# Relative-bias lines of two attention layers: kept with heads innermost, copied DRAM to DRAM, loaded as one run per partition and turned into head order by ScalarE

## What is computed

```
# first block: 16 heads, banded causal attention, window 128
s    = q.k + bias1[head, query - key]           # 128 queries x 256 keys, per block of 128 tokens
bias1[head, d] = rel_bias_table[bucket(d), head]  for 0 <= d < 128, else -1e30
# second block: 8 heads, three branches (compressed, selected, window)
s    = q.k + bias2[head, query - key]           # bucket(d), d < 512
# each block ends in a feed-forward over experts: 128 pairs of rows of two tables per token
```

## Time and profile before

| | |
|---|---|
| time, median of 3 runs | 3303.84 us (3301.78 to 3305.36) |
| the profiled execution | 3307.08 us, of which 3305.4 us are the span from first to last instruction |
| TensorE busy | 2453.2 us (74%) |
| VectorE busy | 2321.0 us (70%) |
| ScalarE busy | 1333.8 us (40%) |
| GpSimd busy | 1137.5 us (34%) |
| moved by DMA | 1295.01 MB, mean 392 GB/s |

### The profile page before, as it was taken

One profiled execution on the slowest core, in us unless ns is written; L12 is line 12 of the kernel. 1 busy time (PEld: TensorE's weight loads), 2 busy tenths in 40 slices (PEclk: granted clock), 3 DMA queues, 4 the chain that ended last, 5 costly groups with the idle time before them and its releaser, 6 DMA issues.

```text
span 3305.4 us, 40579 instructions
## 1 busy us (share of the span) xinstructions
PE 2453.2 (74%) x14052; PEld 1044.4 (32%) x14052; DVE 2321.0 (70%) x5500; ACT 1333.8 (40%) x3603; POOL 1137.5 (34%) x1038
## 2 busy tenths in 40 slices
PE   8969679786797777879688769778876655555555
PEld 3533333223332233346343426423333211111111
DVE  7439783878838787475975685888866777777644
ACT  2114442444424443243483343368733333333322
POOL 0012332324323243332343343444433444443432
PEclk9979879897898978989888979878888777777777
DMA  8899999999999999999999999999999999999997
GB/s 243 310 354 414 412 375 394 411 402 406 382 406 418 412 401 396 408 371 404 369 380 384 386 396 391 408 418 416 385 405 361 414 418 416 417 410 414 420 420 323
DMA packets 214057, 1295.01 MB, mean 392 GB/s; under 512 B 26934, under 2 KB 30294, under 8 KB 82776
## 3 DMA queue, kind: packets, MB, share of 16 engines
q0 software_dynamic: 148320, 1076.50, 80.7%
q1 hardware_dynamic: 64860, 213.81, 17.1%
q10 hardware_dynamic: 672, 2.12, 0.2%
HBM read 1289.62 MB, written 2.71 MB: 391 GB/s over the span
## 4 chain that ended last, share of the span: by engine, by line
PE 34%; DMA 26%; DVE 22%; issue 9%; ACT 5%; POOL 3%; SPq 0%; POOLq 0%; DVEq 0%; ACTq 0%
PE ps L1718 10%; DMA ring<-in_k_vu,idx 10%; PE ps L1798 10%; DMA ring<-in_k_uv,idx 9%; DVE ring L415 9%; DMA wsl<-in_k_wu 5%; PE ps L2092 5%; POOL ring L2396 3%; ACT L1245 2%; PE ps L2102 2%; DVE big L470 2%; PE ps L1775 1%; PE ps L1973 1%; ACT diag L1245 1%; DMA wsl<-in_k_wmod 1%
## 5 line engine op out<-in xcount | busy, mean ns | idle before, releaser
L1718 PE MATMUL ps<-ring,diag 64*64 64x512 f32 x8192 | 1257.7, 742 | 487.3 <-ACT diag L1245 464.4
L415 DVE CUSTOM_DVE_ANT_0 ring<-ring,xn 128x1024 f32<-128x1024 f32 x1024 | 1238.3, 1221 | 480.6 <-DMA ring<-in_k_vu,idx 268.5
L2396 POOL DMA_INDIRECT ring<-in_k_vu,idx x514 | 566.1, 1101 | 1147.0 <-DVE aw L415 663.1
L2396 POOL DMA_INDIRECT ring<-in_k_uv,idx x510 | 565.2, 1108 | 946.3 <-DVE aw L415 674.4
L1718 PEld LDWEIGHTS ps<-ring,diag 64*64 64x64 f32 x8192 | 313.2, 158 | 1259.9 <-ACT diag L1245 739.7
L1245 ACT ACTIVATE aw<-aw 128x2 f32<-128x2 f32 x512 | 104.2, 204 | 1077.1 <-DVE aw L415 1075.8
L1798 PE MATMUL ps<-wsl,xT 128*128 128x512 f32 x896 | 429.2, 622 | 30.5 <-DMA wsl<-in_k_wu 26.5
L1245 ACT ACT_TABLE_LOAD x340 | 436.2, 1283 | 21.2 <-issue 9.3
L1245 ACT ACTIVATE diag<-gid,aw 128x64 f32<-128x64 f32 x1024 | 311.9, 343 | 308.3 <-PE ps L1718 292.3
L1245 ACT ACTIVATE gid<-ident,gate 128x64 f32<-128x64 f32 x1024 | 293.9, 335 | 0.0
L1798 PEld LDWEIGHTS ps<-wsl,xT 128*128 128x128 f32 x896 | 165.7, 196 | 291.9 <-issue 228.3
(11 more groups left out here) (264 smaller groups left out, 2155.2 us busy)
## 6 DMA issues: line engine op xcount, KB each, us to landing
wsl<-in_k_wu SPq DMA_DIRECT2D x342, 512.0 KB, 9.8
wsl<-in_k_wmod SPq DMA_DIRECT2D x40, 512.0 KB, 6.2
ring<-in_k_vu,idx POOLq DMA_INDIRECT x514
ring<-in_k_uv,idx POOLq DMA_INDIRECT x510
ring<-in_k_wmod SPq DMA_DIRECT2D x8, 512.0 KB, 10.4
wsl<-in_k_wu SPq DMA_DIRECT2D x8, 280.0 KB, 19.2
hres<-in_x SPq DMA_DIRECT2D x4, 512.0 KB, 5.9
pers<-L1d POOLq DMA_DIRECT2D x8, 256.0 KB, 15.8
```

The costliest lines, as they stand in the source:

```text
L415: V(v.tensor_tensor_reduce(u_row(s), u_row(s), xn[:, n % 3, :], 1.0, 0.0, ALU.mult, ALU.add, aw[:, b, k:k + 1]), ("dot", s))
L1718: r = t.matmul(PA[half][64 * q:64 * q + 64, :], diag[64 * half:64 * half + 64, s % (2 * PAIR), :], v_row(s)[64 * half:64 * half + 64, 512 ...
L2396: Q(p.indirect_dma_start(out=both_rows(s), out_offset=None, in_=tab, in_offset=bass.IndirectOffsetOnAxis(ap=idx[:, n % 2, k:k + 1], axis=0 ...
```

## The change

The line is now made with distances on the partitions: three matmuls of 128 distances each, heads as columns (so a [128, 3, heads] tile), and the mask is a [128, 3] column tile. The line goes to DRAM once (`lined`, mark `line`), distance by distance with the heads innermost. A second transfer copies it inside DRAM 16 times, end to end (`copied`, rows of 384 x heads). From there the row of a query, all heads, is one contiguous run: 16 KB for block one, 8 KB for block two. Eight transfers of 16 partitions each bring it to `raw1` (scratch in the ring) or `raw2`, key-major with the heads innermost. ScalarE then copies it into `bias1` (four copies of 8 heads x 128 keys, ahead of its evacuation of block b = 3) and `bias2` (two copies of 4 heads x 256 keys, behind the gates of tile pair 4). The loads of `raw1` no longer wait for block b = 3; they start when the copies have landed. VectorE's waits for `bias` become waits for `biased`.

```
-        def shifted(copies, heads, a):
-            return bass.AP(tensor=copies.tensor, offset=128 - 16 * a, ap=[[WC, 16], [16 * WC, heads], [1, 256]])
-        def copied(copies, heads):
-            return bass.AP(tensor=copies.tensor, offset=1, ap=[[16 * WC, heads], [WC + 1, 16], [1, W1]])
+        def shifted(blk, a):
+            nh = (16, 8)[blk]
+            return bass.AP(tensor=copied[blk].tensor, offset=(127 - 16 * a) * nh, ap=[[(W1 - 1) * nh, 16], [1, 256 * nh]])
...
+            def bias_turned(blk, raw, to, h0, k0, nk, part):
+                S.stage("bias")
+                S.wait_ge("bias", blk)
+                S(act(to[:, h0:h0 + 8 - 4 * blk, k0:k0 + nk], raw[:, k0:k0 + nk, h0:h0 + 8 - 4 * blk].rearrange("p k h -> p h k"),
+                      ACT.Copy), ("biased", blk, part))
...
+                    if b == 3:
+                        for part in range(4):
+                            bias_turned(0, raw1, bias1, 8 * (part % 2), 128 * (1 - part // 2), 128, part)
...
-                T(t.matmul(PS[0][0:nh, 0:W1], B["tb"][0:32, 0:nh], B["oh"][0:32, :], start=True, stop=True),
-                  ("bias_mm", blk))
+                for c in range(3):
+                    r = t.matmul(PS[0][:, nh * c:nh * c + nh], B["oh"][0:32, 128 * c:128 * c + 128], B["tb"][0:32, 0:nh],
+                                 start=True, stop=True)
+                T(r, ("bias_mm", blk))
...
-            G.wait_ge("bias_lv", 0)
-            lv = BB[0]["lv"][0:16, 0:W1]
-            Q(p.dma_start(copied(L1d, 16), bc(lv.unsqueeze(1), [16, 16, W1])), "bias_d0", ("bias_d", 0))
-            G.wait_ge("bias_lv", 1)
-            lv = BB[1]["lv"][0:8, 0:W1]
-            Q(p.dma_start(copied(L2d, 8), bc(lv.unsqueeze(1), [8, 16, W1])), "bias_d1", ("bias_d", 1))
+            for blk, nh in ((0, 16), (1, 8)):
+                G.wait_ge("bias_lv", blk)
+                Q(p.dma_start(lined[blk].rearrange("c p h -> p c h"), BB[blk]["lv"][:, :, 0:nh]), "line%d" % blk, ("line", blk))
+            for blk, nh in ((0, 16), (1, 8)):
+                G.wait_ge("line", blk)
+                line = lined[blk].rearrange("c p h -> (c p h)")
+                Q(p.dma_start(copied[blk], bc(line.unsqueeze(0), [16, W1 * nh])), "bias_d%d" % blk, ("bias_d", blk))
             G.wait_ge("bias_d", 0)
-            G.wait_ge("win", 0, 3)
             for a in range(8):
-                Q(p.dma_start(bias1[16 * a:16 * a + 16, :, :], shifted(L1d, 16, a)), "bias0",
-                  *([("bias", 0)] if a == 7 else []))
+                Q(p.dma_start(raw1[16 * a:16 * a + 16, :, :], shifted(0, a)), "bias0", *([("bias", 0)] if a == 7 else []))
...
-                    Y.wait_ge("bias_d", 0)
-                    Y.wait_ge("bias_d", 1)
+                    Y.wait_ge("line", 1)
+                    Y.wait_ge("biased", 0, 3)
...
-                        Q(s.dma_start(bias2[16 * a:16 * a + 16, :, :], shifted(L2d, 8, a)), "bias1",
+                        Q(s.dma_start(raw2[16 * a:16 * a + 16, :, :], shifted(1, a)), "bias1",
```

More of the change, by code:

```diff
@@ L169, in build @@
         iob = bc(iot[:, :].unsqueeze(1).unsqueeze(1), [128, 2, 16, 16])
-        L1d = nc.dram_tensor("L1d", [16, 16, WC], F32, kind="Internal").ap()
-        L2d = nc.dram_tensor("L2d", [8, 16, WC], F32, kind="Internal").ap()
+        lined = [nc.dram_tensor("line%d" % k, [3, 128, nh], F32, kind="Internal").ap() for k, nh in enumerate((16, 8))]
+        copied = [nc.dram_tensor("copies%d" % k, [16, W1 * nh], F32, kind="Internal").ap() for k, nh in enumerate((16, 8))]
         modd = nc.dram_tensor("modd", [12, 512], F32, kind="Internal").ap()
@@ L299, in bias_bufs @@
             r["oh"], o = carve(base, o0, w)
-            r["mk"], o = carve(base, o, w)
+            r["mk"], o = carve(base, o, 3)
             r["tb"], o = carve(base, o, 16)
-            r["lv"], o = carve(base, o, w)
+            r["lv"], o = carve(base, o, 3, 16)
             return r
+        raw1 = carve(rflat, 11264, 256, 16)[0]
+        raw2 = carve(pers, at_route + 256, 256, 8)[0]
         BB = [bias_bufs(rflat, 3328, W1), bias_bufs(rflat, 4608, W1)]
@@ L568, in make_bias @@
                 V.wait_ge("bias_mk", blk)
-                V(tt(B["lv"][0:nh, :], PS[0][0:nh, 0:W1], B["mk"][0:nh, :], ALU.add), ("bias_lv", blk))
+                V(tt(B["lv"][:, :, 0:nh], PS[0][:, 0:3 * nh].rearrange("p (c h) -> p c h", c=3),
+                     bc(B["mk"].unsqueeze(2), [128, 3, nh]), ALU.add), ("bias_lv", blk))
             def norm1(n):
@@ L611, in first_tile @@
                     V.wait_ge("a_sc", 0, e)
-                    V.wait_ge("bias", 0)
+                    V.wait_ge("biased", 0, e)
                     V(tt(sc0[e], both0[e], bias1[:, hs, 128:256], ALU.add))
@@ L684, in att_scores @@
                 V.wait_ge("a_sc", n, g)
-                V.wait_ge("bias", 0)
+                V.wait_ge("biased", 0, 3)
                 for b in range(2):
@@ L1039, in cmp2 @@
                                         PS[4 + g][32 * r_:32 * r_ + 32, 384:448]), *([("vbd", a)] if g * r_ == 3 else []))
-                V.wait_ge("bias", 1)
+                V.wait_ge("biased", 1, 1)
                 for j in range(2):
@@ L1566, in win2 @@
                               *([("we", a, 2)] if j else []))
+                    if b == 2 and not p:
+                        for part in range(2):
+                            bias_turned(1, raw2, bias2, 4 * part, 0, 256, part)
+                            S.stage("win")
                     if b == 3:
@@ L2419, in bias_tables @@
                 load(B["tb"][0:32, 0:nh], tab, "bias_tb", blk)
-                load(B["mk"][0:nh, :], A["k_mask" + sfx], "bias_mk", blk)
+                load(B["mk"], A["k_mask" + sfx], "bias_mk", blk)
             def extra(k):
@@ L2537, in _constants @@
     c["k_rmask"] = (np.arange(128) >= 31).astype(np.float32)[:, None]
-    for nm, w, nh, lim in (("1", W1, 16, 128), ("2", W1, 8, 512)):
+    for nm, w, lim in (("1", W1, 128), ("2", W1, 512)):
         dist = 255 - np.arange(w)
@@ L2545, in _constants @@
         c["k_oh" + nm] = oh
-        c["k_mask" + nm] = np.tile(np.where(ok, 0, NEG).astype(np.float32), (nh, 1))
+        c["k_mask" + nm] = np.where(ok, 0, NEG).astype(np.float32).reshape(3, 128).T
     return c
```

1 line of the change is left out of this document (removed).

## The result

The changed kernel takes 3315.37 us (median of 15 runs, 3310.11 to 3326.49), the kernel before 3303.66 us (15 runs, 3297.05 to 3310.71): a ratio of 1.0037, 95% interval 1.0027 to 1.0047. It is slower by 11.7 us. The profiled execution has a span of 3313.2 us, 7.8 more than before.

What follows compares the result with a forecast made beforehand. It took the prologue's end, which moves the gathers and the end, to bound the kernel. 3307.08 + 9.3 (prologue) - 1.0 (block two) = 3315.4 us profiled; with the median 3.24 below, 3312 us, range 3299 to 3321.

Steps and rivals of the forecast that it cites:

- The price goes with the partitions: Bias loads: a transfer on 16 partitions costs 0.59 us per 4 KB whatever its runs, so longer runs gain nothing.
- Short runs were the price: Rival, bias loads: longer runs cut them to 5 us; gain 5.2 to 8.2 us, 3296 to 3299; chance 0.20.
- the drift between engines: Rival, raw1's loads: engines out of step, loads last 12 to 17 us; 3301 to 3308; chance 0.13 together with ScalarE's rival.
- the two forms of packets: raw1's loads: a 16 KB run as one packet (weights get one unit, to 44.7) or cut into 4 KB (four units, 48.6).
- Landing of the copies near 24: Prologue: two hops of the line through DRAM, 4.5 us each, land near 24 (19 to 28); nothing waits there.
- Unit 9 at 44.7: Prologue: the first weight unit of block b = 2 lands at 44.7 behind raw1's loads, delaying the block's end by 11.4 us.
- The clock, 1.1 us: Prologue, behind the gap in weights: TensorE's clock at the lower level adds 1.1 us to the 11.4 us delay.
- The rival: Stall with ten us at half clock behind it: +13 to +15 us, 3316 to 3319; chance 0.67 together with the forecast stall.
- What comes back, 0.71 us: Prologue, block b = 5: TensorE's wait for a weight unit goes, returning 0.71 us of the 10.0 us delay.
- The lines, 1.9 us: VectorE's set-up: making the lines takes 1.9 us less, but this is lost in the gap.
- ScalarE's copies: Ahead of block b = 3's evacuation: four copies of 1.06 us, 4.2 together, cost nothing even at twice the price.
- Block two, -1.0 us: Block two: TensorE's 2.56 us wait at 1494.75 goes, gathers held up cost 1.6 us; together -1.0 us.

Runs made afterwards that it cites:

- the undisturbed kernel with one transfer: Changed kernel without copies in DRAM, one early transfer over all 128 partitions per load, ScalarE reading backward: 3300.54 us, ratio 0.9985 to before; again 3297.87, 0.9976.
- the single-block runs: Changed kernel with each transfer's 16 partitions 8 apart in one block only: block one 3311.25 us, ratio 1.0015 to before; block two 3310.73, 1.0012.
- both late kernels: Changed kernel with raw1's loads again waiting for block b = 3: 3313.0 us; the same with 16 KB runs cut to 4 KB (block two 2 KB): 3304.05.
- the early cut one: Changed kernel, loads still early, runs cut to 4 KB (block two 2 KB), partitions still neighbours: 3310.27 us, ratio 1.0024 to before.

## Why the prediction was right

It forecast slower, +8.3 us, 3312 us; measured are +11.7 us, 3315.37, inside its range. The mechanism held, with two steps mis-sized that partly cancel, and one term of the wrong sign.

- *The price goes with the partitions.* Right: 0.53 us per 4 KB on 16 neighbours with 16 KB runs, 0.29 eight apart, 0.16 over all. "Whatever its runs" was too strong: cut to 4 KB and beside as many packets of weights it was 0.40. "Short runs were the price" fell with this, and the drift between engines didn't happen. Of the two forms of packets the first (one packet of weights per run) is the nearer: 1.6 a run were measured, where the second wants four.
- *Landing of the copies near 24.* The line took 4.0 us and the copy 3.4; the loads were issued from 22.47 on.
- *Unit 9 at 44.7.* It came at 45.60, and that close partly by luck: the terms erred both ways. The loads were issued from 22.47, not 24.5, and a run took 2.11 us, not 2.36; but 1.6 packets of weights went by per run, not one, and each took 0.56 us, not 0.164. With these numbers the same sum ends at 22.47 + 8 x (2.11 + 1.6 x 0.56) = 46.5, and in the trace q0 has 0.21 MB from 44 to 46 and 0.02 MB from 46 to 48.
- *The clock, 1.1 us.* This step was mis-sized. At the lower level unit 9 took 3.78 us and three more 7.79, together 4.7 us over 1.72 a unit, and 0.98 us of wait lay between. So b = 2 ended at 58.15 instead of 52.7, and VectorE's state-space part began 15.5 us late (59.62 against 44.10), not 10.0. The rival had named 5 us.
- *What comes back, 0.71 us.* It was 3.4: block b = 5 ran 7.13 us at full clock, where before it had 10.5 from 66.33 to its end with the wait, at half clock for about the first half (0.53 to 71.50, 1.00 behind). Another 2.3 us came back between VectorE's start and block b = 5. The scores were 9.8 us late, the first gather 8.6, against a forecast of 9.3.
- *The lines, 1.9 us*, were to be lost in the gap. They were worth less: the first transfer is issued 0.44 us earlier, and in the undisturbed kernel with one transfer VectorE's part begins 0.73 us earlier.
- *ScalarE's copies.* 1.88 us each, not 1.06: nearly the doubling that was allowed for, and hidden as argued. The Trainium skill's note on cachelines ("SBUF — State Buffer", section "Door 1: The DMA port swizzle") has a penalty for such reads. The trace agrees as far as it goes: block two's copies, 32 bytes apart and not 64, took 2.02 us each (4.04 for two); no run read 16 bytes apart or closer but for the contiguous 1.06.
- *Block two, -1.0 us.* The step that failed is "so the unit comes earlier and the 2.56 us go": the wait grew to 4.84 us. Spreading the partitions ends it and short runs shrink it, so both act; why a longer run delays the weights behind it in the same queue no run shows. The charge for the gathers, 1.6 us, was the other term too small: they moved 1.2 MB less in the first 20 us, 5 us at their rate. By the times of the single-block runs block two is worth 5 to 8 us of the 11.7, which is more than its wait, and more than the 3.4 us that the forecast lacks. Block one would then be worth 4 to 7, less than its first gather's delay of 8.6; but the run that moved block one's loads alone lost 0.36%. These intervals overlap, and the split stays open.

## What to carry to other kernels

Before lengthening runs, ask how many partitions each transfer covers: a load over 16 neighbouring partitions took 2.4 to 3.6 times as much of the DMA engines as one over 128 (0.39 to 0.59 us per 4 KB against 0.16), with runs from 1 to 16 KB, and putting its partitions 8 apart (other offsets, the same bytes) took it down to 0.29 to 0.34. Such a load may lie where TensorE stands anyway, and is better not moved to where TensorE consumes weights; and beside a queue that somebody waits for, long contiguous runs leave that queue less than pieces of 4 KB do (0.63 MB against 1.59 in 18 us). Where every partition reads a shifted window of one line, a single overlapping read of the line does the whole job.

## What the runs showed of the hardware, unexpected

- A packet of weights (4 KB, of a unit that spans all partitions) took 0.164 us alone, 0.56 us beside 16 KB runs on neighbours, 0.37 beside 4 KB pieces on neighbours, 0.29 beside 16 KB runs 8 apart, 0.17 beside the single transfer: a transfer on few partitions slows the other queue's packets too, not only their turns.
- For some 6 us, soon after such loads begin, the other queue gets nearly nothing. A unit of weights was issued at 53.43, and from 54 to 58 q0 is all but alone on the engines; both late kernels show the same, at 16 KB and at 4 KB. From 60 on the packets are nearly even the earlier trace rows. The changed kernel has 3 us of it (26 to 29), the early cut one none so clean. Its cause stays open.
- The prologue's clock is a trade. Before, TensorE stood for 2.03 and 1.16 us between 57 and 61 us, waiting for VectorE, and the clock was at 0.50 from 61 to 71. The stall lowered it in b = 2 and left it high in b = 5 (1.00 from 60 to 90 us with early loads on neighbours in runs of 1, 4 and 16 KB alike), and 5.7 of the 15.5 us of VectorE's delay were gone by the scores.
